# Products that nobody reads, placed in front of TensorE's waits between a decoder's attention and its experts

## The reference

```python
k_sh, v_sh = shared_kv(h, kv_norm, w_kv, k_norm, pos)      # 4 kv heads of 64
q = swa_query(rms_norm(h, b_norm), b_w_q, b_q_norm, pos)    # 16 query heads of 64, partly rotated
s = einsum(q, k) * HD ** -0.5                               # blocks of 128 queries, their own and the previous 128 keys
m = max(max(s), sink); p = exp(s - m)
o = einsum(p / (sum(p) + exp(sink - m)), v)
h = h + o @ b_w_o
hn = rms_norm(h, ffn_norm)
top_v, top_i = top_k(hn @ router_w + router_b, 2)           # two experts of eight
h = h + sum over e of combine[e] * ((silu(hn @ w_gate[e]) * (hn @ w_up[e])) @ w_down[e])
```

## Time and profile before

| What | Value |
|---|---|
| Median of three runs | 1588.41 us (1588.24 to 1590.96) |
| The profiled execution's own time | 1588.98 us |
| Its span | 1587.2 us |
| Mean granted clock of TensorE | 0.951 of full speed |
| TensorE busy | 1479.2 us, 93% of the span, 13294 matmul instructions |
| VectorE busy | 900.5 us, 57% |
| ScalarE busy | 648.6 us, 41% |
| GpSimd busy | 208.7 us, 13% |

### The profile page before, as it was taken

The page is one execution under the profiler, slowest core; times in us unless marked ns, Lnnn a source line. Parts: engine busy times, 40 slices in busy tenths (PEclk is TensorE's granted clock), DMA queues, the critical chain, the costliest instruction groups (busy, mean ns, idle before and its releaser), DMA issues. The chain is left out here.

```text
span 1587.2 us, 31920 instructions
## 1 busy us (share of the span) xinstructions
PE 1479.2 (93%) x13294; PEld 1320.5 (83%) x13294; DVE 900.5 (57%) x1197; ACT 648.6 (41%) x1108; POOL 208.7 (13%) x217
## 2 busy tenths in 40 slices
PE   6999989899889999999999998879879999999994
PEld 6999978889889999999999997458867777777773
DVE  5676534755465443444444754543366777676776
ACT  5343534442143222222232413552434565665661
POOL 0111024554011000000011100220011000000002
PEclk8999999999889999999999997889879999999997
DMA  6678240000352323231334530005137888888886
GB/s 177 226 267 280 78 120 2 2 2 3 107 156 72 106 79 106 79 103 57 91 91 131 151 103 21 1 1 134 72 121 240 287 289 294 290 295 268 272 284 239
DMA packets 169741, 226.13 MB, mean 142 GB/s; under 512 B 11272, under 2 KB 134689, under 8 KB 169545
## 3 DMA queue, kind: packets, MB, share of 16 engines
q1 hardware_dynamic: 160246, 191.44, 38.7%
q0 software_dynamic: 8512, 30.48, 5.3%
q10 hardware_dynamic: 862, 2.50, 0.4%
HBM read 188.78 MB, written 37.88 MB: 143 GB/s over the span
## 5 line engine op out<-in xcount | busy, mean ns | idle before, releaser
L276 DVE TENSOR_TENSOR w_lo<-w_raw,w_hi 128x2048 fp32r<-128x2048 f32 (+1 forms) x71 | 153.9, 2172 | 91.4 <-ACT w_hi L268 91.4
L268 ACT ACTIVATE w_hi<-w_raw 128x2048 fp32r<-128x2048 f32 (+1 forms) x71 | 128.1, 1810 | 124.0 <-PE P L221 118.5
L221 PE MATMUL P<-xf_hi,w_hi 128*128 128x260 f32 x704 | 141.8, 282 | 2.0 <-DVEq L1764 1.2
L221 PE MATMUL P<-xf_hi,w_lo 128*128 128x260 f32 x704 | 141.9, 283 | 0.0
L221 PE MATMUL P<-xf_lo,w_hi 128*128 128x260 f32 x704 | 141.7, 283 | 0.0
L221 PEld LDWEIGHTS P<-xf_hi,w_hi 128*128 128x128 f32 x704 | 108.5, 188 | 2.6 <-issue 1.4
L221 PEld LDWEIGHTS P<-xf_hi,w_lo 128*128 128x128 f32 x704 | 108.5, 188 | 0.0
L221 PEld LDWEIGHTS P<-xf_lo,w_hi 128*128 128x128 f32 x704 | 108.2, 188 | 0.0
L221 PE MATMUL P<-xa_hi,w_hi 128*128 128x260 f32 x512 | 104.1, 285 | 2.7 <-DVE xa_lo L319 2.7
L221 PE MATMUL P<-xa_hi,w_lo 128*128 128x260 f32 x512 | 104.1, 285 | 0.0
L221 PE MATMUL P<-xa_lo,w_hi 128*128 128x260 f32 x512 | 103.9, 285 | 0.0
(11 more groups left out here) (553 smaller groups left out, 3320.5 us busy)
## 6 DMA issues: line engine op xcount, KB each, us to landing
raw_more_moe<-in_moe_w_gu_dram SPq DMA_DIRECT2D x64, 512.0 KB, 5.3
w_raw<-in_moe_w_gu_dram SPq DMA_DIRECT2D x64, 512.0 KB, 5.4
w_raw<-in_dense_w_gu_dram SPq DMA_DIRECT2D x44, 512.0 KB, 4.5
expert_out<-zeros POOLq DMA_DIRECT2D x40, 512.0 KB, 4.1
w_raw<-in_a_w_in_dram SPq DMA_DIRECT2D x32, 512.0 KB, 5.0
raw_more_moe<-in_moe_w_down_dram SPq DMA_DIRECT2D x32, 512.0 KB, 4.8
w_raw<-in_moe_w_down_dram SPq DMA_DIRECT2D x32, 512.0 KB, 4.7
w_raw<-in_dense_w_down_dram SPq DMA_DIRECT2D x16, 384.0 KB, 4.0
```

What stands on the lines that cost most here:

```text
L221: ins = nc.tensor.matmul(out[:, b], w, x[:, b * HALF:(b + 1) * HALF], start=(first and n == 0), stop=(last and n == 2))
L268: ins = nc.scalar.activation(hi, raw, ACT.Copy)
L276: ins = nc.vector.tensor_tensor(lo, raw, hi.bitcast(F32), ALU.subtract)
```

## The change

A helper is added that issues products of a constant with itself (the identity, and the first `width` columns of the constants' tile) into a PSUM bank whose content nobody reads. Both operands are plain float32. It is called in seven places of TensorE's program, all in the second layer:

- at the end of the project phase, 5 products of 512 columns, after a wait for ten evacuated tiles;
- in `turn(i)` of attention, 1 product, of 512 columns for items 0 to 3 and of 256 for the others, 16 in all; the two waits for the copies of the item before now stand ahead of it, and the wait for the division behind it;
- after the last `values`, 2 products;
- in front of the wait for `chosen_ready`, 6 products;
- in front of `index(0)`, 2; in front of `turn_x(0)`, 3; behind `turn_x(0)`, 3.

That is 37 products. Nothing is removed.

```diff
+def keep_busy(c, pe, bank, many, width=512):
+    for _ in range(many):
+        pe.matmul(c.P[:, bank, 0:width], cols(c, CI), c.cst[:, 0:width], start=True, stop=True)
...
             turn_and_score(KT - 1).then_inc(logits_ready, 1)
 
+            keep_busy(c, pe, 0, 6)
             pe.wait_ge(chosen_ready, 1)
...
                 pe.wait_ge(round_open, r + 1)
+                keep_busy(c, pe, 0, 2)
                 index(0, 2, 0)
                 index(1, 3, 0)
+                keep_busy(c, pe, 0, 3)
                 turn_x(0)
+                keep_busy(c, pe, 5, 3)
                 for e in range(NE):
...
             side_work("q7")
+            pe.wait_ge(evacuated, 2 * n - 2)
+            keep_busy(c, pe, 0, 5)
...
             def turn(i):
-                pe.wait_ge(divided, i + 1)
                 if i >= 1:
                     pe.wait_ge(placed_act, i)
                 if i > BKV:
                     pe.wait_ge(placed_dve, i - BKV)
+                keep_busy(c, pe, 4, 1, 512 if i < BKV else 256)
+                pe.wait_ge(divided, i + 1)
                 for k in range(blocks(i)):
...
             values(N - 1)
+            keep_busy(c, pe, 4, 2)
```

## The result

The change made the kernel slower. Its median over six runs is 1595.59 us (1589.66 to 1597.18), that of the kernel before, measured beside it, 1589.35 us (1588.24 to 1590.96). The ratio is 1.0032, with a 95% interval from 1.0021 to 1.0043. By the ratio that is 5 us, by the two medians 6.2. The measured median lies beyond the predicted range.

What follows compares the result with a forecast made beforehand. TensorE was taken to bound the experts, and attention to be a four-engine chain slowed by low clock. Terms: 1.0 - 1.6 + 1.3 - 1.2 - 1.2 = -1.7 us, giving 1587.0, range 1580 to 1593.5.

Steps and rivals of the forecast that it cites:

- filler at the low clock: Rival, projection's end and turns: products run at 1.2 GHz and overrun the waits; 5.0 us lost, 1594.0; chance 0.21.
- A: Projection's end, five products: they take 5.9 us against 4.9 idle, so attention starts 1.0 us late.
- B: Attention items 0 to 3: starting at full clock gains 5.0 us, added products cost 3.4; 1.6 us gained.
- The prediction's own sign: Wrong if clock is 1.00 across both long division waits and index, or attention exceeds its 107 by over 3 us.
- part C: Attention items 4 to 15: seven products on the path cost 3.0 us, five hidden, one low stretch saved 1.7: 1.3 lost.
- Part D: After attention, two products: border 0.4 us late, out-projection starts at full clock, saving 1.6; 1.2 us gained.
- Part E: Experts' front: clock falls before the index; delays of 0.8 and 1.6 us, turning and first products faster; 1.2 us gained.
- It doesn't do what it says: Rival, whole kernel: clock falls and rises where it did, filler lies in true idle; 1589; chance 0.08.

Runs made afterwards that it cites:

- e6: Only the 256-column products in the turns of items 4 to 15, against the kernel before: 1594.34 us, ratio 1.0033.
- e1: Only the 16 products in turn(i), with the two waits moved ahead of them, against the kernel before: 1595.18 us, ratio 1.0032.
- e14: Only one 256-column product in each turn of items 6, 8, 9, 12, 13, against the kernel before: 1589.09 us, ratio 0.9994.
- e5: Only the 512-column products in the turns of items 0 to 3, waits in new order, against the kernel before: 1591.39 us, ratio 1.0008.
- e4: Only the 14 products in the experts' front (6, 2, 3, 3), against the kernel before: 1585.36 us, ratio 0.9980.
- e8: Only the experts' front, with four times as many products of 8 columns instead of 512, against the kernel before: 1596.21 us, ratio 1.0039.
- e15: Only 14 products of 8 columns in each turn of items 9 and 13, against the kernel before: 1589.45 us, ratio 0.9995.
- e9: The whole change without the products in turn(i), its waits as before, against the kernel before: 1587.86 us, ratio 0.9977.
- e13: Only one 256-column product in each turn of items 4, 5, 7, 10, 11, 14, 15, against the kernel before: 1592.45 us, ratio 1.0014.
- e11: The front's 14 products, the two after attention and four of 512 columns in turns 9 and 13 each, against the kernel before: 1582.11 us, ratio 0.9958.
- e2: Only the five products at the projection's end, against the kernel before: 1591.22 us, ratio 1.0009.
- e3: Only the two products after the last values, against the kernel before: 1589.46 us, ratio 1.0000.
- e7: No added product, only the three waits of turn(i) in the new order, against the kernel before: 1590.84 us, ratio 1.0001.
- e12: Only the first six products of the experts' front, against the kernel before: 1590.22 us, ratio 1.0003.

## Why the prediction was wrong

The forecast was no change, 1587.0, with a range to 1593.5; 1595.59 was measured. The rival that came nearest is the slower one, filler at the low clock (1594.0), though with another distribution than it gave: it had 3.6 us lost in A and a gain in B, where the trace has 2.1 and a loss. The prediction's own sign fired: from `q7`'s end to the last `values` it is 113.9 us in the changed kernel and 106.1 in the one before, more than 3 us longer.

**The step that failed is part C, "I take one stretch of 3.4 us saved ... 1.3 us lost".** In the trace it lost 4.8, and e6 gives 4.6 over all runs for the same twelve products. Two terms of it were off. The price was 0.43 us for 256 columns by proportion from the rotation, and is 0.53 at the full clock and 1.0 at the low one (0.85 forecast). A single product of 512 columns is 0.96 at the full clock (997.52 to 998.48 in the changed kernel's trace), so the 256 columns more cost 0.43, as forecast, and 0.1 is a fixed part that the proportion left out. Three of the seven on the path (items 4, 11, 14) met the low clock, so the seven cost 4 times 0.53 and 3 times 1.0, 5.1 us, where 3.0 stood. And no stretch was saved: the falls before turns 4, 9 and 13 and within `one3` all came again, and the one at `one3` lasted from 1051 to past 1061 instead of 1050 to 1057. `one3` itself, from 5.2 us to 6.3, took 1.1 of the loss; some 1.4 came back in small pieces at the other places. The bound of the range, 6.0 lost, held; the value taken was too near the favourable side. The saving of one stretch was not impossible: e1's trace has two half stretches saved and loses 1.9 us here. The other half of C was right in kind: e14 shows no cost of the five in the idle. That 0.43 us in front of 3.9 would not hold the clock is what 1037.88 and 1041.84 show, and it was so at six waits of eight, but not at the two of e14.

**Part B, "1.6 us gained", lost 0.9 in the trace**, and e5 puts items 0 to 3 at +1.6 over all runs, at +3.1 in its trace, without A's products. Its largest term was half of `one0`'s 7.0 us. The clock was indeed at 1.00 as attention began, but it fell between 983 and 984 us, just ahead of `one0`, which again took 7.00. The long run of products had ended at 976.1, and what lay between was waits and short products. The favourable end of B, 4.4 us gained, rests on 7.0 us of gains, where the terms that it names, 3.1 and 1.9, give 5.0.

**Part A, "1.0 us late", was 2.1.** The five products took 6.2 us where 5.9 stood. But the slack was not the 4.9 us of the wait row. After the engines meet, ScalarE must still make the mask. The changed kernel, and behind it the kernel before:

```profile
969.89 6.16 PE L221 MATMUL P<-cst 128*128 128x512 f32 x10
```

```profile
976.34 0.63 ACT L2895 ACTIVATE mask_r<-constants_late 128x512 fp32r<-128x512 f32 x1 [3.34 <-PEq L2488]
977.02 0.50 PE L2789 MATMUL P<-mask_r,ident_r 128*128 128x256 f32 x2 [0.96 <-ACT mask_r L2895]
```

```profile
976.18 0.63 ACT L2880 ACTIVATE mask_r<-constants_late 128x512 fp32r<-128x512 f32 x1 [1.27 <-PEq L2477]
976.86 0.80 PE L2776 MATMUL P<-mask_r,ident_r 128*128 128x256 f32 x2 [4.91 <-ACT mask_r L2880]
```

ScalarE's mask starts 0.3 us after the last added product ends, and the first product of attention 0.7 us after that. In the kernel before, that mask starts 0.3 us after VectorE's last reciprocal (974.94 and 0.95). So of the 4.9 us only 3.9 were free to be filled. In the changed kernel they end at 974.0 (970.04 and 3.9), and the last added product ends at 976.05: these are the 2.1 us. The row named the releaser (`mask_r`); what released that in turn had to be looked up too.

**Part D was right in both terms** (0.6 late, 1.5 gained in that trace), and too sure: e4's trace and six others show that the clock can also hold there unaided.

**Part E, "1.2 us gained", was 3.5 in the trace, and 4.2 in e4 (3.2 by the ratio).** The fall that was expected in front of the index came behind it, from 1161 to 1164 us, and an earlier one, from 1147 to 1150, passed within the six products, which took 7.1 us where 5.2 stood. The front of the changed kernel:

```profile
1154.89 1.96 PE L221 MATMUL P<-cst 128*128 128x512 f32 x4
1157.34 3.63 PE L2069 MATMUL P<-constants_late,pick_moe 128*128 128x1 f32 x40 [0.48 <-DVE pick_moe L2335]
1160.90 4.52 PE L221 MATMUL P<-cst 128*128 128x512 f32 x6
1166.54 1.09 PE L2076 MATMUL P<-cst,xb_lo 128*128 128x128 f32 x8 [1.12 <-DMA xb_lo<-token_rows,index]
...
1168.17 2.84 PE L221 MATMUL P<-cst 128*128 128x512 f32 x6
1171.98 0.72 PE L2103 MATMUL P<-more_hi_moe,xb_hi 128*128 128x512 f32 x2 [0.97 <-DVE xb_hi L2368]
```

The index of experts 0 and 1 takes 3.6 us instead of 6.1, the three products behind it fall partly into the low clock (4.5 us instead of 2.8) and still end 1.1 us before the gathered tokens land, because the short index had made room. So neither of the two delays that E charged, 0.8 and 1.6 us, came, and the measured gain is near its favourable end, 4.1. That end counted 0.5 us for a shorter index; it brought nothing: 9.2 us from the first index product to the turning, before and after.

**The rivals.** "It doesn't do what it says" is out: the mean clock rose. The clock did hold in the last part of the front, and there it paid. On the rule of the Trainium skill that transposes do not count ("TensorE: Matmul & The Clock Gate", Part 4): no run here separates transposes from products, so it stays open. What e8 and e15 show is another thing: products with eight columns under which the clock stayed at 0.50 or fell to it.

**Still open.** The parts do not add up exactly: e9 is 0.9977 and the whole change 1.0032, so the turns cost 0.55% on top of e9 and 0.32% alone; e13 and e14 together give 0.08% where e6 gives 0.33%. Since the stretches of low clock lie elsewhere in each kernel, and in part in each execution, a sum of single edits was not to be expected, but which stretch makes up the difference was not settled. Nor was what makes the changed kernel's other executions up to 6 us longer than the one traced.

## What to carry to other kernels

In this kernel products that nobody reads paid only where the wait was about as long as they were at the clock that they met, and where real work on the path followed within a few microseconds. A long wait filled nearly wholly (3.7 of 3.9 us) kept the clock at all four waits seen, one product of 0.5 us at two of eight; that the small one costs nothing there is also shown (e14), that it pays is not. A small product in front of every turn is charged at each place that had no wait, and nearly doubly where the clock is down (1.0 us for 0.53); look up from the timeline which places those are before writing it into a loop. Count the slack from what releases the wait, through the steps that come behind it, and take the filler's price from a start-to-start time, with its fixed part.

## What the runs showed of the hardware that was not expected

The granted clock fell while TensorE was never idle, on products of one to eight columns, as within `one3`. In e8 it stayed at 0.50 over 22.00 busy us. In e11 it fell while TensorE went through its first products for the experts, which of the other traces only e9's has:

```profile
1193.00:1197.00 4.00, 4.00 (x40) 3.63 (x39) 1.33 (x2) 0.37 (x1) 0.00 (x0) 0.97 0.81 241
1197.00:1200.00 3.00, 3.00 (x8) 2.32 (x9) 1.58 (x4) 1.85 (x2) 0.63 (x1) 0.50 0.07 29
```

```profile
1193.47 1.75 PE L2069 MATMUL P<-constants_late,pick_moe 128*128 128x1 f32 x20
1195.15 1.09 PE L2076 MATMUL P<-cst,xb_lo 128*128 128x128 f32 x8
1196.18 0.68 PE L2078 MATMUL P<-cst,xb_lo 32*128 32x32 f32 x8
1196.79 1.22 PE L2103 MATMUL P<-more_hi_moe,xb_hi 128*128 128x512 f32 x2
```

The index products with one column and the narrow turnings (L2069, L2078) precede it; from expert 0's first L2113 to the end of the span e11 took 416.4 us, where the kernel before took 413.7 and all traces but e9's at most 415.1, so part of what the front gained was given back there. The same happened in e9 (416.9), whose clock was low for some 3.4 us between 1203 and 1208.

Identical code differs from execution to execution: everything before `q7`'s end took 968.9 to 973.9 us in the profiled executions of these kernels, although nothing there was changed. What makes that difference was not settled; the time at the low clock in it does not order these traces by length. For a whole kernel the clock tells more: of e9's twelve executions, the five with a mean clock of 0.962 or 0.963 took 1582.9 to 1586.3 us, the seven with 0.958 to 0.961 took 1587.8 to 1590.0, and the traced one is the slowest of them. The runs of one kernel spread accordingly (before: 1586.5 to 1594.5 over all of its runs, e11: 1580.4 to 1587.7); for the small differences (e2, e3, e5, e7, e12, e14, e15) the interval takes in no change at all.
